# Layer 0's modulation rows: all 32 gate quarters on VectorE, in attention's z tiles and heads c

## The chip, the cores and the metric

The kernel runs on one core of one Trainium2 chip. The metric is the device time of one execution in microseconds (us). The kernel before was timed three times: 3288.5, 3288.59 and 3289.92 us, median 3288.59 us.

## The reference

Two blocks follow each other on x, 256 tokens of width D = 2048. The first mixes three gated branches and ends with a feed-forward network (FFN) of width 5504. The second has two layers of attention over 256 latent and 256 context tokens, with three kinds of heads (a, b, c). The part that the change touches is the adaptive modulation:

```python
sc, scc = jax.nn.silu(c), jax.nn.silu(c_ctx)
for l in range(2):
    shift, scale, gate = jnp.split(sc @ w_ada[l] + b_ada[l], 3, axis=-1)
    shift_c, scale_c, gate_c = jnp.split(scc @ w_ada[l] + b_ada[l], 3, axis=-1)
    h = rms(x, norm_w[l]) * (1.0 + scale[:, None]) + shift[:, None]
    hc = rms(xc, norm_w[l]) * (1.0 + scale_c) + shift_c
    ...   # q, k, v and z from h and hc, three attentions
    x = x + gate[:, None] * merge_out(o_a, o_b, o_c, z, w_out[l])
    if l == 0:
        xc = xc + gate_c * merge_out(oa_c, ob_c, oc_c, z_c, w_out[l])
```

So each layer needs two vectors (for c and for c_ctx) times a matrix of 2048 x 6144. Shift and scale of layer 0 are needed before its projections, its gate only in the output projection out0.

## The kernel before, in words

**The weight stream.** All weights lie in DRAM in the order of use, cut into quarters of 128 partitions x 1024 floats (512 KB). SyncE loads quarter n into slot n % 8 of the ring `raw` once TensorE has counted quarter n - 8 as used (`weights_used`). A matmul quarter is split into two fp32r parts before use: ScalarE copies the high part to `whi` (line 844, ring of 4), VectorE subtracts it and writes the low part `wlo` back into the slot (line 1309). Both run 3 quarters ahead (`AHEAD`). TensorE then makes three matmuls per 128 x 128 chunk (lines 2116, 2117 and 2120 in `tile`; in the wide form lines 2143 and 2144).

**The phases** are listed in `PHASES`, each with its number of quarters and of output tiles. Around the change they are: the FFN's rest group, five FFN groups (g = 0 to 4), and for layer 0 z0, a0, za0, b0, zb0, c0, kvb0, qb0 and out0. An FFN group has 16 up tiles of two quarters and 16 down tiles of one. In group 0 GpSimd also prepares the normalised input of the later groups (lines 2747 to 2754), between the up tiles.

**Modulation on TensorE.** Output columns are taken in blocks of 512, 12 blocks per layer; a block is 8 quarters. These quarters are not split: `mod_quarters` takes them straight from `raw`, two after each tile that has some, with silu(c) in 32-column groups as the stationary operand (line 2172). `weave` and the lists `MOD_FEW` (group 0: 16 quarters, blocks 0 and 1) and `MOD_FFN` (groups 1 to 4: 32 quarters each, four blocks) say after which tile they stand. When a block is complete, VectorE copies its rows (line 1724), TensorE transposes them (`mod_fold`, line 2181), and VectorE adds them up and adds the bias (lines 1733 and 1737).

**Modulation on VectorE.** Blocks 10 and 11, the last half of layer 0's gate, are made in phase c0 (heads c): their 16 quarters hold rows instead, that is 128 outputs on the partitions and half of the 2048 inputs along the row. `gate0_products` (line 1810) multiplies such a quarter with silu(c) and with silu(c_ctx), each spread over all partitions in `crow0`, and sums along the row (`tensor_tensor_reduce`, line 1821): two products per quarter, the product itself thrown into PSUM banks 6 and 7. `crow0` holds one half of the inputs; GpSimd loads the first half at the start of layer 0 (line 2785), and the second once 8 quarters are done (its wait on `gate0_mods`). TensorE waits for the products before a tile's last matmul (`rows_made` in `tile`), as only then it counts the slot as used. Layer 1's gate is made in the same way in out0, with the product thrown into SBUF (line 2070).

**za0 and zb0.** These phases make z tiles (6 and 8 of them, 512 wide), and the attention of heads a and b runs between their matmuls. Each z tile has four slots, one after every four chunks. `beside` puts the pairs of heads into slots: 16 pairs in 24 slots, 24 pairs in 32 slots, starting with slot 2. In a pair's slot p, TensorE makes the scores of p (line 2476), the values of p - 2 (line 2502) and the transposes of p - 1 (line 2487). VectorE's order in a slot is in `z_beside`:

```python
if s % 4 == 2 and s > 2: z_done(...)       # line 1953: gate of the z tile before
if p is a pair: maxima(us[p])              # lines 1904 to 1921
lo(pending)                                # line 1309, every other slot
if p >= 2: gated(us[p - 2])                # line 1947
if p is a pair: norms(us[p])               # waits for ScalarE's exp; lines 1932 to 1938
```

ScalarE makes the exponentials (line 1201) after the maxima and copies the transposed probabilities of the pair before (line 1210). Pairs have by turns 512 keys (latent queries) and 256 keys (context queries). With the slots counted from 0, pairs stand in za0 in slots 2, 4, 5, 6, 7, 9, 10, 11, 12, 14, 15, 16, 17, 19, 20 and 21, and in zb0 in 2, 4 to 9, 11 to 16, 18 to 23 and 25 to 29. Pairs of even number are those with 512 keys.

Of the kernel before, what the change touches and what calls it, by code (L numbers as in the profile page):

```python
# [79 lines left out]
MOD_FEW = [0, 2, 0, 0, 2, 0, 0, 2, 0, 0, 2, 0, 0, 2, 0, 0] + [0] * LATE + [2, 0, 0, 2, 0, 0, 2] + [0] * 6  # L80
MOD_GROUPS = [MOD_FEW if g == 0 else MOD_FFN for g in range(FF_GROUPS)]
# [3 lines left out]
def weave(quarters, mods, before=0, lags=(0, 1, 2)):  # L85
# [21 lines left out]
    assert a % 8 == 0  # L107
# [13 lines left out]
MOD_C = [1, 1, 2, 1, 2, 1, 2, 1, 2, 1, 2]  # L121
C_WEAVE = weave([2] * 11, MOD_C)
C_CHUNKS = sum(MOD_C) // 2
# [6 lines left out]
C_BLOCK = 3 * D // 512 - sum(MOD_C) // 8  # L130
BLOCKS = [*range(C_BLOCK), *range(3 * D // 512, 5 * D // 512)]
assert 8 * len(BLOCKS) == sum(map(sum, MOD_GROUPS)) and sum(MOD_OUT) == 2 * KD and not Z_BEFORE

# [41 lines left out]
def _converted():  # L175
# [3 lines left out]
    for name, nq, _ in PHASES:  # L179
# [3 lines left out]
        elif name in ("z0", "z1"):  # L183
            l = int(name[1])
            own = {pos for e in Z_WEAVE[l] for pos, _ in e["pre"] + e["mods"]}
        elif name in ("c0", "out0"):
            own = {pos for e in (C_WEAVE if name == "c0" else OUT_WEAVE) for pos, _ in e["mods"]}
# [66 lines left out]
def build(nc, stream, xT, ctxT, params, consts, natten, out):  # L254
# [24 lines left out]
    region("gate_mod", 3 * KD * 4)  # L279
# [51 lines left out]
    gate0_half = sb("gate0_half", [2, C_CHUNKS], F32, "gate_mod", 2 * KD * 4)  # L331
# [33 lines left out]
    with ExitStack() as ctx:  # L365
# [225 lines left out]
        def projections(name, l):  # L591
# [700 lines left out]
        def _(vec):  # L1292
# [517 lines left out]
            def gate0_products(e):  # L1810

                for pos, a in e["mods"]:
                    s, (half_, t) = Q0["c0"] + pos, divmod(a, C_CHUNKS)
                    j = 4 * C_BLOCK + t
                    vec.wait_ge(crow0_in, 16 * (half_ + 1))
                    vec.wait_ge(raw_in[s % SLOTS], 16 * (s // SLOTS + 1))
                    for c in range(2):
# [3 lines left out]
                        last = vec.tensor_tensor_reduce(psum[:, 6:8, :].rearrange("p b c -> p (b c)"), raw[:, s % SLOTS, :],  # L1821
# [9 lines left out]
            def projected(name, l):  # L1831
                tiles_, items = projections(name, l)
                for u, (s, nq) in enumerate(t[0:2] for t in tiles_):
                    if name == "a" and l and Z_PAIRS + u <= KD // 2:
                        pair(JOBS_OF["hc1"][0], Z_PAIRS + u)
                    if name == "c" and l == 0 and u < len(C_WEAVE):
                        gate0_products(C_WEAVE[u])

# [118 lines left out]
            def z_beside(kind, l, carry):  # L1957
# [5 lines left out]
                for s in range(4 * n):  # L1963
# [135 lines left out]
        def _(pe):  # L2099
# [4 lines left out]
            def tile(s, d, ts, td, cat, c0, loff, width, nq=2, nch=8, k0=0, ready=None, beside_=None, rows=(), rows_made=None):  # L2104
# [4 lines left out]
                for q in range(nq):  # L2109
# [3 lines left out]
                    for k in range(nch):  # L2113
# [4 lines left out]
                        if rows and q == nq - 1 and k == nch - 1:  # L2118
                            pe.wait_ge(rows_made, rows[-1][1] + 1)
# [279 lines left out]
            def projected(name, l):  # L2399
                tiles_, items = projections(name, l)  # L2400
                first = T0[f"{name}{l}"]
                for u, (s, nq, nch, cat, k0, w) in enumerate(t[0:6] for t in tiles_):
# [9 lines left out]
                    if name == "c" and u == 23:  # L2412
                        cat_ready(JOBS_OF[f"cq{l}"][0])
                    rows = C_WEAVE[u]["mods"] if name == "c" and l == 0 and u < len(C_WEAVE) else ()
                    tile(SQ.index(s), 0, first + u, 0, cat, 0, 2 * S, w, nq=nq, nch=nch, k0=k0, ready=ready,
                         rows=rows, rows_made=gate0_mods)
# [96 lines left out]
            def z_beside(kind, l, carry):  # L2513
# [145 lines left out]
        def _(pool):  # L2659
# [133 lines left out]
            for l in range(LAYERS):  # L2793
# [12 lines left out]
                if l == 0:  # L2806
                    pool.wait_ge(gate0_mods, C_CHUNKS)
# [28 lines left out]
def _stream(w):  # L2836
# [16 lines left out]
    rows = w["w_ada_2"][:, :, 2 * D:].reshape(LAYERS, KD, P, KD, P).transpose(0, 3, 4, 2, 1).reshape(LAYERS, KD, P, 2, QW)  # L2853
# [145 lines left out]
```

## Time and profile before

| what | value |
|---|---|
| median of the runs | 3288.59 us |
| the profiled execution, its time | 3289.74 us |
| its span in the profile | 3287.6 us |
| mean granted TensorE clock | 0.999 of full speed |
| ScalarE, GpSimd busy | 1431.3 us, 614.2 us |
| DMA | 557.67 MB, 170 GB/s mean |
| phases (us from the start of the span) | FFN group 0: 869 to 1006; za0: 1798 to 1897; zb0: 2021 to 2162; c0: 2162 to 2285 |

A row of a timeline has the start, the length, the engine, the line, the operation with output and inputs, a count where several are merged, and in brackets the idle time of the engine before it with what ended it. A row of windows has the stretch, its length, then the busy us (with the number of instructions) of TensorE's matmuls, TensorE's weight loads, VectorE, ScalarE and GpSimd, and last TensorE's granted clock (1.00 is 2.4 GHz, 0.50 is 1.2 GHz), the busy share of DMA and its GB/s. PE is TensorE, DVE VectorE, ACT ScalarE and POOL GpSimd. Matmuls are pipelined, so a matmul's length is longer than the distance to the next.

### The profile page before, as it was taken

Reading aid. Unit: us, or ns where it says so; the run is one execution under the profiler, and the core shown is the slowest. Engines: PE = TensorE matmul, PEld = TensorE weight load, DVE = VectorE, ACT = ScalarE, POOL = GpSimd, SP = SyncE. Lnnn points to the kernel's source line nnn. Section 1 sums busy time; section 2 is a strip of 40 time slices with the busy share of each in tenths; the row PEclk is TensorE's granted clock in tenths of the full one; section 3 lists DMA queues with packets and bytes.
Section 4 is the critical chain, followed back from the end, with each engine's and each line's share of the span. In section 5 each row is a group of like instructions: output and inputs, shape, how many; then the busy total and the mean of one; then the engine's idle time right before and its main releaser. Section 6 shows DMA issues by size and latency. Waiting matters only on the chain.

```text
span 3287.6 us, 56246 instructions
## 1 busy us (share of the span) xinstructions
PE 3251.8 (99%) x20418; PEld 2783.6 (85%) x20418; DVE 2240.7 (68%) x3318; ACT 1431.3 (44%) x2193; POOL 614.2 (19%) x550
## 2 busy tenths in 40 slices
PE   8999999999999999999999999999999999999999
PEld 8999999998987777788888787777868888888978
DVE  7887877567877677677765566567657666774665
ACT  5444445444443343444543433532352363543353
POOL 4999930111440000000300000000001100000000
PEclk9999999999999999999999999999999999999999
DMA  6555555565567777777732222134326533322235
GB/s 219 185 180 183 185 184 185 186 212 182 203 232 253 282 265 279 255 273 263 273 108 101 72 88 78 58 109 148 108 80 214 204 132 111 137 90 96 94 107 171
DMA packets 159583, 557.67 MB, mean 170 GB/s; under 512 B 17520, under 2 KB 23808, under 8 KB 159232
## 3 DMA queue, kind: packets, MB, share of 16 engines
q1 hardware_dynamic: 154144, 534.67, 47.1%
q0 software_dynamic: 5216, 19.94, 1.8%
q8 instruction: 151, 2.47, 0.3%
q14 instruction: 72, 0.59, 0.1%
HBM read 548.23 MB, written 6.31 MB: 169 GB/s over the span
## 4 chain that ended last, share of the span: by engine, by line
PE 94%; DVE 3%; ACT 1%; issue 1%; DVEq 1%; ACTq 0%; DMA 0%; POOL 0%; SPq 0%
PE psum L2116 18%; PE psum L2120 18%; PE psum L2117 18%; PE psum L2143 15%; PE psum L2144 7%; PE psum L2327 4%; PE psum L2476 2%; PE psum L2502 2%; PE psum L2172 2%; PE psum L2487 2%; PE psum L2328 2%; DVE wlo L1309 1%; PE psum L2247 1%; PE psum L2433 1%; DVE rst L1340 0%
## 5 line engine op out<-in xcount | busy, mean ns | idle before, releaser
L844 ACT ACTIVATE whi<-raw 128x1024 fp32r<-128x1024 f32 (+3 forms) x844 | 864.8, 1030 | 1033.7 <-PE psum L2120 571.8
L1309 DVE TENSOR_TENSOR wlo<-raw,whi 128x1024 fp32r<-128x1024 f32 (+3 forms) x844 | 1035.5, 1233 | 398.6 <-ACT whi L844 370.5
L2116 PE MATMUL psum<-hcat,whi 128*128 128x256 f32 (+1 forms) x3436 | 1126.7, 328 | 7.1 <-DVE wlo L1309 6.4
L2120 PE MATMUL psum<-hcat,wlo 128*128 128x256 f32 (+1 forms) x3436 | 1110.6, 323 | 0.0
L2117 PE MATMUL psum<-hcat,whi 128*128 128x256 f32 (+1 forms) x3436 | 1110.4, 323 | 0.0
L2143 PE MATMUL psum<-hcat,whi 128*128 128x512 f32 x2048 | 727.1, 399 | 0.1
L2116 PEld LDWEIGHTS psum<-hcat,whi 128*128 128x128 f32 x3436 | 654.4, 190 | 75.7 <-issue 19.0
L2120 PEld LDWEIGHTS psum<-hcat,wlo 128*128 128x128 f32 x3436 | 654.3, 190 | 51.5
L2117 PEld LDWEIGHTS psum<-hcat,whi 128*128 128x128 f32 x3436 | 654.8, 191 | 49.2 <-issue 0.7
L2144 PE MATMUL psum<-hcat,wlo 128*128 128x256 f32 x2048 | 573.5, 280 | 0.0
L2143 PEld LDWEIGHTS psum<-hcat,whi 128*128 128x128 f32 x2048 | 384.5, 188 | 114.6 <-issue 25.6
L2144 PEld LDWEIGHTS psum<-hcat,wlo 128*128 128x128 f32 x2048 | 386.6, 189 | 0.1
L2675 POOL TENSOR_SCALAR tap<-glu,par 128x255 f32<-128x255 f32 (+9 forms) x150 | 203.6, 1357 | 0.3 <-issue 0.3
L2327 PE MATMUL psum<-thirdcat,whi 128*128 128x512 f32 x512 | 182.4, 400 | 0.0
L2662 POOL TENSOR_TENSOR thirdcat<-tmp,thirdcat 128x256 fp32r<-128x256 f32 x43 | 51.3, 1193 | 634.0 <-ACT thirdcat L898 634.0
L2677 POOL TENSOR_TENSOR conv<-conv,tap 128x255 f32<-128x255 f32 (+9 forms) x150 | 149.3, 995 | 22.1 <-issue 0.3
L2328 PE MATMUL psum<-thirdcat,wlo 128*128 128x256 f32 x512 | 142.8, 279 | 0.0
L2327 PEld LDWEIGHTS psum<-thirdcat,whi 128*128 128x128 f32 x512 | 96.1, 188 | 39.6 <-issue 12.6
L2714 POOL TENSOR_TENSOR racc<-racc,rsq 128x256 f32<-128x256 f32 (+1 forms) x64 | 82.8, 1294 | 236.0 <-ACT rsq L910 209.7
L1340 DVE RECIPROCAL rst<-rst 128x512 f32<-128x512 f32 (+1 forms) x39 | 106.8, 2738 | 27.4 <-ACT rst L873 27.4
L1855 DVE COPY qkv<-psum 128x512 f32<-128x512 f32 (+1 forms) x78 | 49.5, 635 | 111.3 <-PE psum L2120 111.2
L1913 DVE TENSOR_REDUCE stat<-psum 128x2 f32<-128x1024 f32 x78 | 81.6, 1046 | 34.2 <-PE psum L2476 30.2
(297 smaller groups left out, 3568.2 us busy)
## 6 DMA issues: line engine op xcount, KB each, us to landing
raw<-in_stream SPq DMA_DIRECT2D x978, 512.0 KB, 4.3
raw<-in_stream SPq DMA_DIRECT2D x18, 384.0 KB, 3.0
raw<-in_stream SPq DMA_DIRECT2D x24, 256.0 KB, 2.6
resid_dram<-X POOLq DMA_DIRECT2D x2, 2048.0 KB, 9.1
bias<-in_natten POOLq DMA_DIRECT2D x16, 256.0 KB, 3.0
X<-resid_dram POOLq DMA_DIRECT2D x4, 1024.0 KB, 6.1
raw<-in_stream SPq DMA_DIRECT2D x16, 192.0 KB, 2.4
crow<-c_dram POOLq DMA_DIRECT2D x3, 1024.0 KB, 7.3
```

Source lines behind the costliest of these rows:

```text
L844: act.activation(whi[:, c % HI_SLOTS, 0:n], raw[:, slot, 0:n], ACT.Copy).then_inc(hi_ready, 1)
L1309: vec.tensor_tensor(wlo[:, slot, 0:n], raw[:, slot, 0:n], whi[:, c % HI_SLOTS, 0:n].bitcast(F32), ALU.subtract).then_inc(lo_ready, 1)
L1340: vec.reciprocal(r, r)
L2116: pe.matmul(dst, h, cat[:, kk, c0:c0 + width], start=(q == 0 and k == 0), stop=False)
L2117: pe.matmul(dst, h, cat[:, kk, c0 + loff:c0 + loff + width], start=False, stop=False)
L2120: last = pe.matmul(dst, l_, cat[:, kk, c0:c0 + width], start=False, stop=(q == nq - 1 and k == nch - 1))
L2143: pe.matmul(psum[:, bank, :].rearrange("p (l c) -> p l c", l=2), h, both, start=first, stop=False)
L2144: return pe.matmul(psum[:, bank, 0:S], l_, both[:, 0, :], start=False, stop=last)
L2327: pe.matmul(psum[:, bank, :], h, thirdcat[:, kk, :], start=first, stop=False)
L2328: return pe.matmul(psum[:, bank, 0:S], l_, thirdcat[:, kk, 0:S], start=False, stop=last)
L2675: pool.tensor_scalar(tap[:, t % 2, 0:S - t], pick(glu, c, 0, S - t), wt, None, ALU.mult)
L2677: pool.tensor_tensor(pick(conv, c, t, S), pick(conv, c, t, S), tap[:, t % 2, 0:S - t], ALU.add)
```

## The change

The whole gate of layer 0 (blocks 8 to 11, 32 row quarters) is now made by `gate0_products`: 8 quarters in za0, 8 in zb0, and 16 in c0 as before. The first 16 use the first half of the inputs, the 16 of c0 the second. FFN group 0 has no modulation quarters; blocks 0 to 3 are in group 1, 4 to 7 in group 2, 12 to 19 in groups 3 and 4 as before. The number of quarters in the stream stays the same.

In `z_beside` a tile's first row quarter is taken in slot 4t + 1 and its second, where there is one, in slot 4t + 2, after `gated` and before `norms`. The product is thrown into the last two chunks of X in SBUF, which the z tiles fill last. GpSimd waits for 16 quarters instead of 8 before it loads the second half. `ctx_extra` has one more fence (a drain of VectorE) before `gains(0)`.

```diff
-MOD_FEW = [0, 2, 0, 0, 2, 0, 0, 2, 0, 0, 2, 0, 0, 2, 0, 0] + [0] * LATE + [2, 0, 0, 2, 0, 0, 2] + [0] * 6
-MOD_GROUPS = [MOD_FEW if g == 0 else MOD_FFN for g in range(FF_GROUPS)]
+MOD_GROUPS = [[0] * len(MOD_FFN) if g == 0 else MOD_FFN for g in range(FF_GROUPS)]
...
-MOD_C = [1, 1, 2, 1, 2, 1, 2, 1, 2, 1, 2]
-C_WEAVE = weave([2] * 11, MOD_C)
-C_CHUNKS = sum(MOD_C) // 2
+ROW_MODS = dict(za0=[1, 1, 2, 1, 2, 1], zb0=[1] * 8, c0=[1, 1, 2, 1, 2, 1, 2, 1, 2, 1, 2])
+ROW_WEAVE = {name: weave([2] * len(m), m) for name, m in ROW_MODS.items()}
...
+ROW_BLOCKS = [*range(2 * D // 512, 3 * D // 512)] + [5 * D // 512 - 2, 5 * D // 512 - 1]
+ROW_BLOCKS = ROW_BLOCKS[4 - min(ROW_CHUNKS // 4, 4):ROW_CHUNKS // 4 if ROW_CHUNKS > 16 else 4]
+ROW_OF = [4 * b + i for b in ROW_BLOCKS for i in range(4)]
+BLOCKS = [b for b in _blocks if b not in ROW_BLOCKS]
...
             def ctx_extra(t):
                 m = t - 2 * FF_GROUP
                 if t == 0:
+                    fence()
                     gains(0)
...
-            def gate0_products(e):
-
-                for pos, a in e["mods"]:
-                    s, (half_, t) = Q0["c0"] + pos, divmod(a, C_CHUNKS)
-                    j = 4 * C_BLOCK + t
+            def gate0_products(name, e, out, some=slice(None)):
+
+                for pos, a in e["mods"][some]:
+                    s, (half_, t) = Q0[name] + pos, divmod(ROWS0[name] + a, ROW_CHUNKS)
+                    j = ROW_OF[t]
                     vec.wait_ge(crow0_in, 16 * (half_ + 1))
                     vec.wait_ge(raw_in[s % SLOTS], 16 * (s // SLOTS + 1))
                     for c in range(2):
                         start = gate0_half[:, c, t:t + 1] if half_ else pv("b_ada", j)
                         total = ada_t[:, c, j:j + 1] if half_ else gate0_half[:, c, t:t + 1]
                         fence()
-                        last = vec.tensor_tensor_reduce(psum[:, 6:8, :].rearrange("p b c -> p (b c)"), raw[:, s % SLOTS, :],
+                        last = vec.tensor_tensor_reduce(out.rearrange("p b c -> p (b c)"), raw[:, s % SLOTS, :],
                                                         crow0[:, c, :], 1.0, start, ALU.mult, ALU.add, total)
                     last.then_inc(gate0_mods, 1)
...
                     if p is not None and p >= 2:
                         gated(us[p - 2])
+                    if name in ROW_WEAVE and s % 4 in (1, 2):
+                        gate0_products(name, ROW_WEAVE[name][s // 4], X[:, KD - 2:KD, :], slice(s % 4 - 1, s % 4))
                     if p is not None and p < len(us):
                         norms(us[p])
...
+                    rows = ROW_WEAVE[name][t]["mods"] if name in ROW_WEAVE else ()
                     tile(C0[name] + 2 * t, 0, T0[name] + t, 0, hcat, 0, 2 * S, chunks_w(l),
-                         beside_=lambda h: slot(4 * t + h))
+                         beside_=lambda h: slot(4 * t + h), rows=rows, rows_made=gate0_mods, made=ROWS0.get(name, 0))
...
-                    pool.wait_ge(gate0_mods, C_CHUNKS)
+                    pool.wait_ge(gate0_mods, ROW_CHUNKS)
                     crow0_load(1)
```

## Rows read from the trace of the kernel before

**Rows 1.** Busy time of each engine over the whole span, from the page.

```profile
PE 3251.8 (99%) x20418; PEld 2783.6 (85%) x20418; DVE 2240.7 (68%) x3318; ACT 1431.3 (44%) x2193; POOL 614.2 (19%) x550
```

**Rows 2.** Windows: FFN's first group, za0, zb0 (busy us by engine, clock, DMA).

```profile
869.00:1006.00 137.00, 137.00 (x1010) 123.10 (x1010) 110.66 (x163) 57.12 (x76) 54.55 (x52) 1.00 0.69 233
1798.00:1897.00 99.00, 99.00 (x610) 72.29 (x609) 56.17 (x119) 45.96 (x98) 3.23 (x6) 1.00 0.23 75
2021.00:2162.00 141.00, 141.00 (x883) 102.32 (x882) 83.35 (x201) 74.98 (x192) 0.00 (x0) 1.00 0.17 57
```

**Rows 3.** Timeline of TensorE, first group: a pair of modulation quarters between two tiles.

```profile
906.58 0.28 PE L2120 MATMUL psum<-hcat,wlo 128*128 128x256 f32 x1
906.79 1.06 PE L2172 MATMUL psum<-raw,cs 128*32 128x512 f32 x8
...
908.01 0.28 PE L2117 MATMUL psum<-hcat,whi 128*128 128x256 f32 x1
```

**Rows 4.** Timeline of TensorE, first group: a fold between two tiles.

```profile
950.44 0.28 PE L2120 MATMUL psum<-hcat,wlo 128*128 128x256 f32 x1
950.56 0.60 PE L2181 MATMUL psum<-con,arow 128*128 128x128 f32 x4
...
951.11 0.28 PE L2117 MATMUL psum<-hcat,whi 128*128 128x256 f32 x1
```

**Rows 5.** VectorE: line 2070's products (min/median/max ns), and two quarters' products in heads c.

```profile
L2070 DVE CUSTOM_DVE_ANT_0 row_product<-raw,crow,par x16: 1284/1285/2086, 2459.5 to 2595.5; 128x1024 f32<-128x1024 f32 x16
...
2209.43 1.29 DVE L1821 CUSTOM_DVE_ANT_0 psum<-raw,crow,par 128x1024 f32<-128x1024 f32 x1
...
2212.38 1.29 DVE L1821 CUSTOM_DVE_ANT_0 psum<-raw,crow,par 128x1024 f32<-128x1024 f32 x1
```

**Rows 6.** Timeline of VectorE in za0, slots 5, 9 and 10.

```profile
1817.50 0.17 DVE L1934 RECIPROCAL stat<-stat 128x2 f32<-128x2 f32 x1 [1.32 <-ACT probs L1201]
1817.75 0.88 DVE L1938 TENSOR_SCALAR probs<-probs,stat 128x512 f32<-128x512 f32 x2
...
1834.06 0.16 DVE L1934 RECIPROCAL stat<-stat 128x2 f32<-128x2 f32 x1
...
1834.82 0.68 DVE L1953 SCALAR_TENSOR_TENSOR X<-tmp,psum 128x512 f32<-128x512 f32 x1
1837.31 0.70 DVE L1904 SCALAR_TENSOR_TENSOR psum<-bias,psum 128x512 f32<-128x512 f32 x1 [1.80 <-PE psum L2476]
...
1841.41 0.17 DVE L1934 RECIPROCAL stat<-stat 128x2 f32<-128x2 f32 x1 [0.19 <-ACT probs L1201]
1841.66 0.88 DVE L1938 TENSOR_SCALAR probs<-probs,stat 128x512 f32<-128x512 f32 x2
```

**Rows 7.** Timeline of VectorE in zb0, slots 5 and 26.

```profile
2040.54 0.16 DVE L1932 TENSOR_TENSOR stat<-stat 128x2 f32<-128x2 f32 x1 [1.36 <-ACT probs L1201]
...
2041.01 0.88 DVE L1938 TENSOR_SCALAR probs<-probs,stat 128x512 f32<-128x512 f32 x2
...
2138.62 0.43 DVE L1911 TENSOR_TENSOR psum<-psum,con 128x256 f32<-128x256 f32 x1 [1.35 <-PE psum L2476]
```

**Rows 8.** Timeline of TensorE: the transposes that read the probabilities of those pairs.

```profile
1819.21 1.09 PE L2487 MATMUL psum<-con,probs 128*128 128x128 f32 x8
...
1842.77 1.09 PE L2487 MATMUL psum<-con,probs 128*128 128x128 f32 x8
...
2042.15 1.09 PE L2487 MATMUL psum<-con,probs 128*128 128x128 f32 x8
```

**Rows 9.** Timeline of TensorE in z1: its longest wait.

```profile
2648.14 0.58 PE L2116 MATMUL psum<-hcat,whi 128*128 128x256 f32 x1 [3.26 <-DVE wlo L1309]
```

**Rows 10.** Windows right behind that wait; columns as in rows 2.

```profile
2648.00:2654.00 6.00, 5.86 (x28) 5.86 (x29) 5.21 (x7) 3.88 (x8) 0.00 (x0) 0.52 0.03 8
2654.00:2660.00 6.00, 6.00 (x52) 6.00 (x51) 3.69 (x5) 5.62 (x10) 0.00 (x0) 1.00 0.52 175
```

**Rows 11.** Line 2785, loads of crow0: issue to landing.

```profile
DMA to landing us min/median/max: 7.3/9.5/11.6
```

More of the change, by code:

```diff
@@ L120 @@
 Z_PAIRS = 4
-MOD_C = [1, 1, 2, 1, 2, 1, 2, 1, 2, 1, 2]
-C_WEAVE = weave([2] * 11, MOD_C)
-C_CHUNKS = sum(MOD_C) // 2
+ROW_MODS = dict(za0=[1, 1, 2, 1, 2, 1], zb0=[1] * 8, c0=[1, 1, 2, 1, 2, 1, 2, 1, 2, 1, 2])
+ROW_WEAVE = {name: weave([2] * len(m), m) for name, m in ROW_MODS.items()}
+ROWS0, _n = {}, 0
+for _name, _m in ROW_MODS.items():
+    ROWS0[_name] = _n
+    _n += sum(_m)
+ROW_CHUNKS = _n // 2
 MOD_OUT = [0] + [2, 2, 3, 2, 2, 3, 2, 2, 3, 2, 2, 3, 2, 2] + [0]
@@ L185, in _converted @@
             own = {pos for e in Z_WEAVE[l] for pos, _ in e["pre"] + e["mods"]}
-        elif name in ("c0", "out0"):
-            own = {pos for e in (C_WEAVE if name == "c0" else OUT_WEAVE) for pos, _ in e["mods"]}
+        elif name in ROW_WEAVE or name == "out0":
+            own = {pos for e in ROW_WEAVE.get(name, OUT_WEAVE) for pos, _ in e["mods"]}
         of += [Q0[name] + k for k in range(nq) if k not in own]
@@ L1835, in projected @@
                         pair(JOBS_OF["hc1"][0], Z_PAIRS + u)
[L1836 to L1837 removed]
+                    if name == "c" and l == 0 and u < len(ROW_WEAVE["c0"]):
+                        gate0_products("c0", ROW_WEAVE["c0"][u], psum[:, 6:8, :])
                     if u < len(tiles_) - 1 or name != "c":
@@ L2102, in weight, with tile @@
                 return whi[:, c % HI_SLOTS, col:col + n], wlo[:, SQ[c] % SLOTS, col:col + n]
-            def tile(s, d, ts, td, cat, c0, loff, width, nq=2, nch=8, k0=0, ready=None, beside_=None, rows=(), rows_made=None):
+            def tile(s, d, ts, td, cat, c0, loff, width, nq=2, nch=8, k0=0, ready=None, beside_=None, rows=(), rows_made=None, made=0):
                 pe.wait_ge(psum_free, FREE[ts] + td)
@@ L2118, in tile @@
                         if rows and q == nq - 1 and k == nch - 1:
-                            pe.wait_ge(rows_made, rows[-1][1] + 1)
+                            pe.wait_ge(rows_made, made + rows[-1][1] + 1)
                         last = pe.matmul(dst, l_, cat[:, kk, c0:c0 + width], start=False,
@@ L2413, in projected @@
                         cat_ready(JOBS_OF[f"cq{l}"][0])
-                    rows = C_WEAVE[u]["mods"] if name == "c" and l == 0 and u < len(C_WEAVE) else ()
+                    rows = ROW_WEAVE["c0"][u]["mods"] if name == "c" and l == 0 and u < len(ROW_WEAVE["c0"]) else ()
                     tile(SQ.index(s), 0, first + u, 0, cat, 0, 2 * S, w, nq=nq, nch=nch, k0=k0, ready=ready,
-                         rows=rows, rows_made=gate0_mods)
+                         rows=rows, rows_made=gate0_mods, made=ROWS0["c0"])
                 return items[len(tiles_):]
@@ L2862, in put_woven, with put_rows @@
                 put(mods[a_])
+    def put_rows(name, tiles_):
+        if name in ROW_WEAVE:
+            put_woven(ROW_WEAVE[name], tiles_, rows_c[ROWS0[name]:])
+        else:
+            put(tiles_)
     for g in range(-1, FF_GROUPS):
```

33 lines of the change are left out of this document (16 added, 17 removed).

## The prediction

> **What bounds the kernel now.** I read the page first: TensorE is busy for 99% of the span and VectorE for 68% [rows 1], so only what TensorE does or waits for can count. The windows come next, since an average hides stages. In the three stretches that the change touches, TensorE is busy all the time at a granted clock of 1.00, while VectorE works 110.66 of 137 us in the FFN's first group, 56.17 of 99 in za0 and 83.35 of 141 in zb0 [rows 2]. The timelines then show what the spare time of VectorE is made of: in the attention stages it is a relay. TensorE writes scores, VectorE takes maxima, ScalarE exponentials, VectorE normalises (lines 1934 to 1938), and TensorE transposes the result one slot later. VectorE's idle time stands in front of its own parts of the relay [rows 6, 7], and what matters is how long before the transposes [rows 8] it is done.
>
> **What TensorE loses as work.** Blocks 10 and 11 of the modulation leave the first group for line 1821 (its two blocks fall away, as the others shift through the groups). That is 16 quarters, sent in 8 pairs. Around a pair, the third matmul starts 1.43 us after the last of the tile before; at the 0.12 us pitch seen between neighbours [rows 4] it would be 0.24, so a pair costs 1.19 [rows 3], and 8 cost 9.5. A fold costs 0.67 - 0.24 = 0.43 [rows 4], two cost 0.9. **Gain: 10.4 us**, all on the path, as TensorE never idles there.
>
> **What could give some of it back in the first group.** VectorE keeps 110.66 us there less four small mod operations per block (nothing taken for them), in 137 - 10.4 = 126.6 us: 87% instead of 81%. It stays below full, and low halves are made three quarters ahead, which covers single late ones. GpSimd's 54.55 us [rows 2] is squeezed as well, and is far from full. I take 0.3. Below, nothing; above, 3.3, the longest wait of TensorE for a low half that the trace has [rows 9]. DMA demand in the group only falls.
>
> **What VectorE gains as work.** Sixteen more quarters (two products each), 8 in za0 and 8 in zb0. The count in heads c is unchanged. Two products with their fences take 2212.38 - 2209.43 = 2.95 us there, with the result thrown into PSUM; where it goes to SBUF, as now everywhere in attention, one product is 1.285 us [rows 5], so two are at least 2.57. I take 2.95, as it includes fences and accumulator reads. Sum: 47.2 us of work, 23.6 per stage, into 42.8 and 57.7 us of idle. It would fit by sum, so placement decides: each quarter's products stand in slots 4t+1 (and 4t+2 for a tile's second), after the gating and right in front of the normalising of that slot's pair. I walk through the slots.
>
> za0 (24 slots; products in 1, 5, 9, 10, 13, 17, 18, 21):
> - Slot 1 precedes the first pair; slot 13 holds no pair; in slots 17 and 18 the slot without a pair behind takes them up; in 9 and 21 the pair has 256 keys and was ready early. No cost by themselves.
> - Slot 5: VectorE idled 1.32 us before the normalising, so this ends 2.95 - 1.32 = 1.63 later; it ended at 1817.75 + 0.88 = 1818.63 [rows 6] and was wanted at 1819.21 [rows 8]. Slack 0.58, **wait 1.05**.
> - Slots 9 and 10, back to back: in 9 there was no idle, so everything moves by 2.95. The z gating that follows starts at 1837.77 and takes 0.68 and a fence (0.81), so the next maxima start at 1838.58 instead of 1837.31: 1.27 late. Then slot 10's products: 1.27 + 2.95 - 0.19 of idle = 4.03 late, with 1842.77 - 1842.54 = 0.23 of slack [rows 6, 8]. **Wait 3.8**, the largest single one.
>
> zb0 (32 slots; products in 1, 5, 9, 13, 17, 21, 25, 29):
> - Slots 5 and 21: 2.95 - 1.36 = 1.59 late, slack 2042.15 - 2041.89 = 0.26 [rows 7, 8]: **1.33 each**.
> - Slot 25 delays slot 26's maxima, before which VectorE idled 1.35: 1.6 late, slack again 0.26: **1.34**.
> - Slot 13 leaves some 0.2 for slot 14 in the same manner; 1, 9, 17 and 29 nothing (first, or followed by a slot without a pair, or a pair of 256 keys).
>
> Together 4.85 + 4.2 = **9.1 us of new waits** of TensorE. With 2.57 per quarter the same walk gives 6.3.
>
> **Other edits.** In both stages the rows are woven into the weight ring: three quarters per z tile (about 17 us) instead of two, 8 slots, and DMA at 0.23 and 0.17 of its capacity [rows 2]. SyncE's queue issues as many loads as before, 16 of them later, so I cost it at nothing; were this cover gone, ScalarE's copies would start late, at a load's length per tile. TensorE waits for the products before a tile's last matmul, half a tile after they are made: nothing. GpSimd's second load of crow0 now waits for zb0's last product (slot 29) and lands 7.3 us later, at most 11.6 [rows 11]. Two slots of 141/32 = 4.4 us follow slot 29, so it lands before heads c begins or at most some 3 us into it, and TensorE asks for the first products only at the end of a tile that takes longer: nothing. Behind that wait on GpSimd stands the crow load, wanted much later. One fence before gains(0): nothing.
>
> **Sum.** -10.4 + 0.3 + 9.1 = -1.0 us. The profiled execution took 3289.74 us and would take 3288.7; the median of the runs, 3288.59, lies 1.15 lower, and I predict against it: **3287.6 us**. The bounds: 6.3 of waits and no loss in the first group give 3284.5; 3.3 lost there gives 3290.6.
>
> **Rivals.**
> - *The wait of 3.8 us lowers the clock.* After TensorE's longest wait, 3.26 us [rows 9], the granted clock in the next 6 us is 0.52, its lower level of 1.2 GHz for most of it, and 28 matmuls start where 52 do in the 6 us behind [rows 10]. That is 6 - 28 x 6/52 = 2.8 us lost. Slot 10 may do the same: 3287.6 + 2.8 = 3290.4. Against it: the wait is only worked out, and smaller if products are cheaper. The Trainium skill, "TensorE: Matmul & The Clock Gate", section "What's actually happening", says the same in general: the low clock is the default, recent activity releases it. The trace agrees at 0.52. By that rule the time would be this rival's.
> - *VectorE's idle covers the products (faster).* If the relay bends (the 42.8 and 57.7 us are enough by sum) only slot 10 costs something, 2 us: 3288.6 - 10.4 + 2 = 3280. Against it: slacks of 0.23 to 0.58 us.
> - *The lateness is handed on (slower).* Late maxima make ScalarE's exponentials late, these the next scores, so that lateness is not worked off before the next product. Then nine products (slots 5, 9, 10, 21 and 5, 13, 21, 25, 29) cost their whole 2.95: 26.6 of waits, 3288.6 - 10.4 + 26.6 = 3304.8. It ends slower from 17 us of waits on, that is once six products cost in full. Against it: a z tile has 7.1 us of VectorE idle on average, more than one product pair.
> - *The work leaves the first group without its time.* VectorE turns out to set the pace there, and half of the 10.4 stays: 3292.8.
>
> **How the numbers follow.** Forecast 0.42, lower clock 0.27, covered 0.14, handed on 0.12, first group keeps its time 0.05. The first two and the last stay within 0.2% (6.6 us, about what a measurement of this kernel can tell from no change): same 0.74, faster 0.14, slower 0.12. The likeliest case's own range is 3284.5 to 3290.6. The range is stretched towards the covered case below and, past the lower clock with the upper bounds (3293.4), partly towards the handed-on one: 3281 to 3297.
>
> **What would show it.** In the first group no line 2172 or 2181, and some 127 us where there were 137. In za0 and zb0, line 1821 sixteen times two, near 1.29 us each, and waits of TensorE for line 1938 or 1201, one of them near 3.8 us in za0's slot 10, and the granted clock right behind it. za0 longer by about 5 us and zb0 by about 4, heads c unchanged. I am wrong if these stages grow by under 4 or over 17 us together, or if the first group shrinks by under 8.

## The result, and the profile after

The changed kernel takes 3293.85 us (median of 20 runs), the kernel before 3288.56 us (20 runs beside it): a ratio of 1.0015 with a 95% interval of 1.0009 to 1.0021. That is 5.3 us slower. It is inside the 0.2% that the prediction takes for no change and inside its range of 3281 to 3297, but clear of noise and on the other side of the forecast of 1.0 us faster. The profiled execution took 3294.27 us, its span is 3292.4 us, and its mean granted clock is 0.997 (0.999 before). The medians here and below are of fast runs, without two slow ones of e_defer, of 7858.9 and 11268.82 us.

Busy time over the span, from the page of the changed kernel:

```profile
PE 3246.4 (99%) x20346; PEld 2785.5 (85%) x20346; DVE 2277.1 (69%) x3372; ACT 1431.3 (43%) x2193; POOL 615.6 (19%) x550
```

TensorE is busy for 5.4 us less than in [rows 1], about half of the work that left it, and VectorE for 36.4 more. The three stretches of [rows 2], each with the start it has here and the length that was forecast, in windows of the changed kernel (columns as there):

```profile
869.00:996.00 127.00, 127.00 (x942) 121.16 (x941) 108.29 (x152) 57.10 (x77) 54.70 (x52) 1.00 0.54 184
1790.00:1894.00 104.00, 96.22 (x557) 69.10 (x555) 67.45 (x136) 42.70 (x91) 3.23 (x6) 0.95 0.29 102
2018.00:2163.00 145.00, 142.23 (x875) 103.16 (x874) 101.53 (x228) 72.80 (x186) 0.00 (x0) 1.00 0.24 82
```

The first group is what was forecast: TensorE full, VectorE 85% busy (87% was forecast). In zb0 TensorE idles for 2.8 us. The surprise is za0: it idles for 7.8 us there, and the clock is 0.95. TensorE's waits in the changed kernel, longest sums first:

```profile
PE psum L2279 <- DVE wlo L1320: 10.0, 1, 10.0
PE psum L2134 <- DVE gate_half L1833: 7.0, 2, 3.7
PE psum L2130 <- DVE wlo L1320: 6.4, 4, 3.3
PE psum L2501 <- DVE probs L1950: 5.5, 8, 1.1
PE psum L2490 <- ACT probs L1212: 2.6, 3, 1.0
```

The first and third are as old as the kernel. The second is new, and it is the wait that the prediction costed at nothing: line 2134 is a tile's matmul on the low half (2120 before), line 1833 the row product. Its two places, in the timeline of TensorE:

```profile
1834.23 0.39 PE L2131 MATMUL psum<-hcat,whi 128*128 128x512 f32 x1
1838.32 0.77 PE L2134 MATMUL psum<-hcat,wlo 128*128 128x512 f32 x1 [3.70 <-DVE gate_half L1833]
...
1877.34 0.39 PE L2131 MATMUL psum<-hcat,whi 128*128 128x512 f32 x1
1880.98 0.47 PE L2134 MATMUL psum<-hcat,wlo 128*128 128x512 f32 x1 [3.25 <-DVE gate_half L1833]
```

And what VectorE did meanwhile, in its timeline:

```profile
1832.54 1.23 DVE L1925 TENSOR_REDUCE stat<-psum 128x2 f32<-128x1024 f32 x1
...
1835.47 1.28 DVE L1833 CUSTOM_DVE_ANT_0 X<-raw,crow,par 128x1024 f32<-128x1024 f32 x1
1836.68 0.08 DVE L1833 DVE_READ_ACCUMULATOR2_ANT gate_half<- 128x1 f32 x1
1836.88 1.28 DVE L1833 CUSTOM_DVE_ANT_0 X<-raw,crow,par 128x1024 f32<-128x1024 f32 x1
1838.09 0.08 DVE L1833 DVE_READ_ACCUMULATOR2_ANT gate_half<- 128x1 f32 x1
1838.09 0.16 DVE L1946 RECIPROCAL stat<-stat 128x2 f32<-128x2 f32 x1
```

Tile 2 has two row quarters, in slots 9 and 10. TensorE had put out the scores of slot 10 and gone straight on to the tile's last matmuls (the last stands just ahead of slot 11). VectorE finished the maxima of slot 10 at 1834.0, when TensorE was all but there (1834.6), and then made a low half, gated, and had the quarter's products still to do. A quarter's products in slot 4t+2 are made while TensorE is already at the end of the tile. In slot 18 (tile 4) it is the same. Behind both stops the granted clock goes down, in windows of the changed kernel:

```profile
1838.00:1844.00 6.00, 5.68 (x24) 4.12 (x25) 3.07 (x11) 1.79 (x5) 0.00 (x0) 0.52 0.61 225
1844.00:1850.00 6.00, 6.00 (x40) 4.19 (x40) 2.49 (x4) 2.05 (x4) 0.10 (x1) 1.00 0.10 40
1881.00:1887.00 6.00, 6.00 (x30) 4.42 (x31) 2.87 (x7) 2.76 (x7) 0.00 (x0) 0.72 0.66 239
1887.00:1893.00 6.00, 6.00 (x40) 4.20 (x39) 3.56 (x6) 2.34 (x6) 0.00 (x0) 1.00 0.07 26
```

At the full clock 40 matmuls start in 6 us, in the two low windows 24 and 30: 6 - 24 x 6/40 = 2.4 us and 6 - 30 x 6/40 = 1.5 us are lost. That count sets unlike mixes of matmuls side by side. By the granted clock itself it would be 6 x (1 - 0.52) = 2.9 us and 6 x (1 - 0.72) = 1.7 us, the first less some 0.2 for the end of the stop, which lies in its window. So the clock costs 3.9 to 4.4 us in za0, as an estimate. How long the stages take is best read from the first and the last matmul of one kind. The scores of the kernel before (minimum, median and longest in ns, then first and last start), in za0 and in zb0:

```profile
L2476 PE MATMUL psum<-qkv x64: 376/534/693, 1801.4 to 1889.0; 64*128 64x512 f32 x32, 64*128 64x256 f32 x32
...
L2476 PE MATMUL psum<-qkv x96: 376/534/693, 2024.3 to 2153.6; 64*128 64x512 f32 x48, 64*128 64x256 f32 x48
```

The same of the changed kernel:

```profile
L2490 PE MATMUL psum<-qkv x64: 376/589/792, 1793.7 to 1893.7; 64*128 64x512 f32 x32, 64*128 64x256 f32 x32
...
L2490 PE MATMUL psum<-qkv x96: 376/534/693, 2029.0 to 2161.5; 64*128 64x512 f32 x48, 64*128 64x256 f32 x48
```

za0's scores took 87.6 us and take 100.0: **12.4 us longer**, where 4.85 was forecast. zb0's took 129.3 and take 132.5: **3.2 us longer**, where 4.2 was forecast. And za0 starts 7.7 us earlier, not 10.1. The sum of these three terms is +7.9; the spans differ by 4.8, and the last 3.1 come back behind zb0, in stages that the change doesn't touch.

The missing 2.4 us of the FFN have their own story. TensorE waits for GpSimd once just ahead of the FFN, 2.2 us in every kernel here. Windows behind that wait, first of the kernel before:

```profile
843.00:849.00 6.00, 5.96 (x49) 5.96 (x50) 5.11 (x11) 4.70 (x13) 4.29 (x6) 1.00 0.52 172
```

then of the changed kernel:

```profile
843.00:849.00 6.00, 6.00 (x39) 6.00 (x40) 4.95 (x11) 3.94 (x10) 3.94 (x6) 0.72 0.40 135
```

The clock fell in one and not in the other. What the experiments say of that stands below.

### The profile page after: what moved, and what is told of

It is laid out like the page before. It is cut to its first block, busy times and chain, and to the rows that moved or that the text cites. A ratio compares the mean times of both kernels' runs of the same rounds, so it can differ in the third digit from the quotient of the medians.

```text
span 3292.4 us, 56207 instructions
## 1 busy us (share of the span) xinstructions
PE 3246.4 (99%) x20346; PEld 2785.5 (85%) x20346; DVE 2277.1 (69%) x3372; ACT 1431.3 (43%) x2193; POOL 615.6 (19%) x550
## 4 chain that ended last, share of the span: by engine, by line
PE 91%; DVE 5%; ACT 2%; DVEq 1%; issue 1%; ACTq 0%; DMA 0%; POOL 0%; SPq 0%
PE psum L2130 17%; PE psum L2134 17%; PE psum L2131 17%; PE psum L2157 15%; PE psum L2158 7%; PE psum L2341 4%; PE psum L2490 2%; PE psum L2516 2%; PE psum L2186 2%; PE psum L2342 2%; PE psum L2501 2%; DVE wlo L1320 1%; DVE X L1833 1%; PE psum L2261 1%; DVEq L1306 1%
## 5 line engine op out<-in xcount | busy, mean ns | idle before, releaser
L1212 ACT ACTIVATE probs<-psum,stat 128x512 f32<-128x512 f32 (+1 forms) x120 | 72.5, 606 | 78.2 <-DVE stat L1931 78.2
```

## The experiments

**Theory 1** was: the products of a tile's second row quarter make TensorE stop at the tile's last matmul; each stop also lowers the clock; the remaining waits are the ones that the prediction walked through. Its rivals were that the lateness is paid wherever TensorE waits, and that the ring and the queues, not the products, make the time. All kernels start from the changed one. The kernel before was run beside them each time and had medians of 3290.92 us (e_gain, e_short, e_defer, e_both), 3289.55 (e_again, e_one, e_free) and 3289.79 (e_free_own), so the ratios, and not the times, can be set side by side. The table takes its times, read to 0.1 us, from the same rows for each: "FFN" is from the first matmul of the line at which the 2.2 us wait stands (2370, 2356 before; 838.5 in the kernel before, so the wait itself is inside) to the first scores of za0, "group" from that matmul to the first group's last down matmul, za0 and zb0 from first to last scores, and the clock is that of the window 843 to 849.

| kernel | ratio to before (95%) | clock | group | FFN | za0 | zb0 |
|---|---|---|---|---|---|---|
| before | 1 | 1.00 | 166.9 | 962.9 | 87.6 | 129.3 |
| changed | 1.0015 (1.0009 to 1.0021) | 0.72 | 158.3 | 955.4 | 100.0 | 132.5 |
| e_again | 1.0015 (1.0006 to 1.0024) | 0.72 | 158.2 | 955.4 | 100.0 | 132.4 |
| e_gain | 0.9969 (0.9958 to 0.9980) | 0.72 | 158.2 | 954.7 | 87.6 | 129.3 |
| e_short | 0.9972 (0.9961 to 0.9983) | 0.72 | 158.3 | 954.5 | 88.3 | 129.3 |
| e_defer | 0.9997 (0.9988 to 1.0006) | 1.00 | 156.8 | 953.0 | 94.2 | 132.4 |
| e_both | 0.9995 (0.9986 to 1.0004) | 1.00 | 156.8 | 953.6 | 93.8 | 132.4 |
| e_one | 0.9984 (0.9975 to 0.9993) | 0.72 | 158.1 | 954.3 | 89.2 | 132.7 |
| e_free | 0.9968 (0.9956 to 0.9980) | 0.72 | 158.2 | 954.4 | 87.5 | 129.8 |
| e_free_own | 1.0029 (1.0019 to 1.0038) | 0.72 | 158.2 | 954.6 | 99.7 | 136.9 |

**e_gain: the FFN's part alone.**

```diff
-ROW_MODS = dict(za0=[1, 1, 2, 1, 2, 1], zb0=[1] * 8, c0=[1, 1, 2, 1, 2, 1, 2, 1, 2, 1, 2])
+ROW_MODS = dict(za0=[0] * 6, zb0=[0] * 8, c0=[1, 1, 2, 1, 2, 1, 2, 1, 2, 1, 2])
...
-BLOCKS = [b for b in _blocks if b not in ROW_BLOCKS]
+BLOCKS = [b for b in _blocks if b not in range(8, 12)]
...
+            vec.memset(ada_t[:, :, 32:40], 0.0)
```

> The changed kernel without any row product in za0 and zb0: blocks 8 and 9 of the modulation (half of layer 0's gate) are left out and read as zeros, so that the 16 quarters leave the FFN's first group and come back nowhere. Theory 1 (the FFN gives 7.7 us, as the start of za0 moved in the changed kernel's trace; everything over that is lost in za0 and zb0): 3280.9 us, with za0 and zb0 as long as in the kernel before. Theory 2 (the FFN gives the predicted 10.1 to 10.4 us, and some of it is given back only because the new loads wait in SyncE's queue): 3278.3 us. In both the granted clock stays at 1.00 in za0.

Measured: 3280.13 us beside 3290.92 for the kernel before, a ratio of 0.9969, that is 10.2 us less, nearer to theory 2's number (the ratios; by the spans of the two profiled executions it is 8.1). za0 and zb0 are as long as before, with no new wait. The trace shows both theories half right: the first group saves 8.7 us (166.9 to 158.2), and the window behind the 2.2 us wait shows the low clock. In e_defer and e_both, where that window shows 1.00, the group saves 10.1. So the FFN gives 10.1 us, as predicted, and an execution whose clock falls there loses 1.5 of them again. Up to 1.1 more goes between the first group and za0 (FFN less group: 797.1 in the changed kernel, 796.0 before). In the changed kernel most of it stands at three quarters whose first matmul starts late, at 1434.27, 1467.76 and 1473.88, 0.34 to 0.40 us behind its neighbour instead of 0.12; in e_free all three start in step. In e_again and e_both a wait of 0.94 and 0.71 us for GpSimd's queue at 1626 (0.23 elsewhere) is part of it. Why they are late isn't shown.

**e_short: products over 64 of 1024 columns.**

```diff
-                        last = vec.tensor_tensor_reduce(out.rearrange("p b c -> p (b c)"), raw[:, s % SLOTS, :],
-                                                        crow0[:, c, :], 1.0, start, ALU.mult, ALU.add, total)
+                        m_ = QW if name == "c0" else 64
+                        last = vec.tensor_tensor_reduce(out.rearrange("p b c -> p (b c)")[:, 0:m_], raw[:, s % SLOTS, 0:m_],
+                                                        crow0[:, c, 0:m_], 1.0, start, ALU.mult, ALU.add, total)
```

> Every row product in za0 and zb0 stays where it is, with its loads, fences and TensorE's waits for it, but covers 64 of its 1024 columns (the rest of those 16 sums is left out). Theory 1 (the waits are made by VectorE's time in the products): no wait of TensorE over 0.5 us for the products, clock 1.00, some 3282 us, 1 us over the kernel without any products. Rival (the ring and the queues, that is 16 more quarters in these stages, or the semaphore waits themselves, make the time): 3288 us or more, with za0 still at least 6 us longer than before.

Measured: 3281.12 us, ratio 0.9972. One stop for the products is left, 0.5 us, in slot 10, and za0 is 0.7 us longer than before. The 16 extra quarters in the ring, their loads, the fences and the waits cost at most that in za0, and nothing in zb0. The rival falls: it is VectorE's time that costs.

**e_defer: TensorE waits for a tile's products half a tile later.**

```diff
+                        if late_rows and q == 0 and k == nch - 1:
+                            pe.wait_ge(rows_made, made + late_rows[-1][1] + 1)
...
-                            last.then_inc(weights_used, 1 + (len(rows) if q == nq - 1 else 0))
+                            last.then_inc(weights_used, 1 + (len(rows) if q == nq - 1 else 0) + (len(late_rows) if q == 0 else 0))
...
-                    rows = ROW_WEAVE[name][t]["mods"] if name in ROW_WEAVE else ()
+                    rows = ROW_WEAVE[name][t]["mods"] if name in ROW_WEAVE and t == n_ - 1 else ()
+                    late_rows = ROW_WEAVE[name][t - 1]["mods"] if name in ROW_WEAVE and t else ()
```

> TensorE's wait for a tile's row products stands at the end of the next tile's first quarter instead of before the tile's own last matmul; nothing is left out. Theory 1 (the stops of 3.70 and 3.25 us come from that place, and each lowers the clock for some 5 us, which costs 2.4 to 2.8): slot 18's stop and its low clock go, slot 10's becomes a wait of about 3.1 us at the transposes: 3288 us if the clock still falls there, 3285.3 if it doesn't. Rival (the relay is late by the same amount and TensorE meets it wherever it waits): the waits stand at the transposes instead, both of them, and the time stays at 3293 to 3294 us.

The ring slots of the row quarters are given back half a tile later as well. Measured: 3289.62 us, ratio 0.9997, 5.9 us less than the changed kernel (by the ratios). za0 fell from 100.0 to 94.2. The waits of TensorE that are left in za0, in its timeline:

```profile
1811.37 1.09 PE L2503 MATMUL psum<-con,probs 128*128 128x128 f32 x8 [0.82 <-DVE probs L1950]
1834.47 0.70 PE L2492 MATMUL psum<-qkv 64*128 64x256 f32 x4 [0.71 <-ACT probs L1212]
1838.20 1.97 PE L2503 MATMUL psum<-con,probs 128*128 128x128 f32 x8 [2.43 <-DVE probs L1950]
```

Slot 18's stop is gone and nothing stands in its place: it was the wait's position alone. Slot 10's became 0.71 + 2.43 = 3.1 us at scores and transposes, as theory 1 had it, and the clock fell behind it. Windows of e_defer:

```profile
1837.00:1843.00 6.00, 4.80 (x16) 4.13 (x17) 2.80 (x11) 3.48 (x7) 0.00 (x0) 0.50 0.00 0
1843.00:1849.00 6.00, 6.00 (x39) 4.18 (x38) 3.20 (x5) 1.07 (x3) 0.54 (x1) 0.96 0.01 3
```

The rival (same time, other place) falls for slot 18. For slot 10 most of the time is indeed paid in another place, 3.1 of 3.70 us, as theory 1 had it too.

**e_both: both products of a tile in slot 4t+1.**

```diff
-                    if name in ROW_WEAVE and s % 4 in (1, 2):
-                        gate0_products(name, ROW_WEAVE[name][s // 4], X[:, KD - 2:KD, :], slice(s % 4 - 1, s % 4))
+                    if name in ROW_WEAVE and s % 4 == 1:
+                        gate0_products(name, ROW_WEAVE[name][s // 4], X[:, KD - 2:KD, :])
```

> Both row quarters of a two-quarter tile (za0's slots 9 and 17) in slot 4t+1, none in 4t+2; TensorE's wait as in the changed kernel. Theory 1: the products are done before the tile's last matmul, so TensorE doesn't stop there; slot 17 has no pair of its own behind it and costs under 1 us, slot 9 delays its pair by 5.7 us, a wait of 2 to 4.5 us at transposes, with a low clock behind it if it is over 3: 3284 to 3289 us. Rival (lateness is only moved and is paid in full in either place): 3292 to 3296 us.

Measured: 3288.99 us, ratio 0.9995, inside theory 1's range, at its upper end. Two waits take the place of slot 10's stop, in TensorE's timeline:

```profile
1833.16 0.66 PE L2501 MATMUL psum<-con,probs 128*128 128x128 f32 x4 [2.35 <-DVE probs L1950]
...
1837.68 0.70 PE L2490 MATMUL psum<-qkv 64*128 64x256 f32 x4 [1.11 <-ACT probs L1212]
```

and slot 17 still makes TensorE stop at the last matmul, for 1.4 us, where the expectation had no stop and under 1 us. With slot 5's 0.83 that is 5.7 of the 6.2 us that za0 grew by. The clock didn't fall this time, in windows of e_both:

```profile
1832.00:1838.00 6.00, 3.72 (x19) 2.87 (x20) 5.30 (x13) 1.82 (x5) 0.54 (x1) 1.00 0.12 16
1838.00:1844.00 6.00, 6.00 (x40) 3.97 (x38) 2.66 (x9) 3.48 (x8) 0.00 (x0) 1.00 0.72 289
```

So 3.1 us of waits within a few us lowered the clock in e_defer, and 3.5 us of them didn't here. What tells these two apart is left open. The 3 us that the expectation set for a low clock is no mark: the clock fell behind waits of 2.2 and 1.6 us elsewhere (below) and stayed up behind one of 3.25.

**e_again: the changed kernel once more.**

> The changed kernel once more, on the chip of the other experiments. Theory: the low clock right at the FFN's start (one stretch of a granted clock of 0.5, 1.5 us lost) comes and goes between executions, the two low stretches in za0 come every time, as both follow the kernel's own stops: 1.0015 times the kernel before again, +4 to +6 us, za0 longer by 12.4 us and zb0 by 3.2. Rival (za0's low clock was that execution's chance, too): za0 longer by 7 to 8 us only, and the time within 1 us of the kernel before.

Measured: 3294.05 us, ratio 1.0015. za0's stops are 3.71 and 3.25 us with the same two low stretches behind them. The rival falls: they come with the kernel. The low clock ahead of the FFN came again too, so that "comes and goes between executions" isn't shown for this kernel.

**e_one: one row quarter per z tile, 18 in heads c.**

```diff
...
-ROW_MODS = dict(za0=[1, 1, 2, 1, 2, 1], zb0=[1] * 8, c0=[1, 1, 2, 1, 2, 1, 2, 1, 2, 1, 2])
+ROW_MODS = dict(za0=[1] * 6, zb0=[1] * 8, c0=[2, 0, 2, 2, 2, 1, 2, 2, 2, 1, 2])
```

> One row quarter per z tile (6 in za0, 8 in zb0) and 18 in heads c, with the second half of crow0 loaded between heads c's first and third tile; nothing is left out. Theory 1 (second products of a tile make the stops): za0 costs 0.8 us (slot 5), zb0 3.2 as before, clock 1.00 in both, no stop of TensorE for the products; with -10.1 in the FFN the kernel before less 6: ratio 0.998. Rival (heads c becomes the place that pays: crow0 lands after VectorE asks for it, or two products a tile are too many): TensorE waits there, 3 us or more, and the ratio is 0.999 or over.

Measured: 3285.48 us, ratio 0.9984, that is 5.3 us less than the kernel before, where 6 were expected. No stop for the products. za0 pays 0.83 in slot 5 and 0.70 behind slot 9 (the second wasn't expected), zb0 its three waits of 0.80, 0.80 and 0.96. Heads c takes 18 quarters without a new wait.

**e_free: products where the relay has nothing to do.** To e_defer's edit comes

```diff
...
+ROW_MODS = dict(za0=[2, 0, 1, 1, 2, 1], zb0=[2, 0, 1, 1, 1, 0, 1, 1], c0=[2, 0, 2, 2, 2, 1, 2, 2, 2, 1, 2])
+ROW_SLOTS = dict(za0=[1, 3, 8, 13, 17, 18, 21], zb0=[1, 3, 9, 13, 17, 24, 29])
...
-                    if name in ROW_WEAVE and s % 4 in (1, 2):
-                        gate0_products(name, ROW_WEAVE[name][s // 4], X[:, KD - 2:KD, :], slice(s % 4 - 1, s % 4))
+                    if name in ROW_WEAVE and s in ROW_SLOTS[name]:
+                        i = ROW_SLOTS[name].index(s)
+                        gate0_products(name, dict(mods=[m for e in ROW_WEAVE[name] for m in e["mods"]]), X[:, KD - 2:KD, :],
+                                       slice(i, i + 1))
```

> The row products stand where VectorE's relay has no pair, or a pair of 256 keys: slots 1, 3, 8, 13, 17, 18, 21 of za0 and 1, 3, 9, 13, 17, 24, 29 of zb0; 18 quarters in heads c; TensorE's wait at the end of the next tile's first quarter. Nothing is left out. Theory 1 (only the place of the products costs, not their 47 us of work): no new wait of TensorE in za0 and zb0, under 0.5 us each, all of the FFN's 10.1 us kept: ratio 0.997. Rival (the idle time of neighbouring slots is needed by the relay itself, so that lateness is handed on): 3 us or more of waits at transposes and scores, ratio 0.998 or over.

Measured: 3279.28 us beside 3289.55 for the kernel before, ratio 0.9968 (0.9956 to 0.9980): **10.3 us faster than before and about 15 faster than the changed kernel**, with nothing left out. Windows of e_free: za0, zb0, and heads c.

```profile
1790.00:1894.00 104.00, 104.00 (x636) 76.06 (x635) 74.25 (x148) 47.45 (x100) 3.23 (x6) 1.00 0.32 106
2010.00:2160.00 150.00, 149.59 (x927) 108.92 (x926) 105.00 (x238) 77.04 (x195) 0.00 (x0) 1.00 0.24 82
2157.00:2262.00 105.00, 105.00 (x460) 85.54 (x457) 76.73 (x99) 27.27 (x32) 0.71 (x1) 1.00 0.51 177
```

In za0 TensorE is busy for 104.00 of 104 us at a clock of 1.00, where the changed kernel shows 96.22 at 0.95. The 28 products of za0 and zb0 cost 0.5 us in all (zb0: 129.3 to 129.8, one wait of 0.31). e_one has the same 14 quarters in za0 and zb0 and the same 18 in heads c, so the places and TensorE's wait alone make these two stages 4.6 us longer there (89.2 + 132.7 beside 87.5 + 129.8).

Not all of the 10.3 us is the change's. By the last scores of zb0 e_free is 6.2 us ahead of the kernel before (2147.4 and 2153.6), although it starts the FFN 1.8 us later and loses 1.5 to the low clock there. The other 4.1 come where no edit reaches: some 2.2 in z1, where the clock stayed at 1.00 behind [rows 9]'s stop (the prediction worked out a loss of 2.8 us from [rows 10]), and 1.6 in the last 90 us. The stages that the edits touch give 8.1: the FFN 8.5 (10.1 less the clock's 1.5), less 0.4 in za0 and zb0.

**e_free_own: the same slots, TensorE's wait back before the tile's own last matmul.**

```diff
-                    rows = ROW_WEAVE[name][t]["mods"] if name in ROW_WEAVE and t == n_ - 1 else ()
-                    late_rows = ROW_WEAVE[name][t - 1]["mods"] if name in ROW_WEAVE and t else ()
+                    rows = ROW_WEAVE[name][t]["mods"] if name in ROW_WEAVE else ()
```

> The slots of e_free, with TensorE's wait for a tile's products put back before that tile's own last matmul (just ahead of slot 4t+3); nothing is left out. Theory 1 (TensorE stops for every product that stands in slot 4t+2 or later of its tile, one slot ahead of VectorE): exactly three stops, for the products in slots 3 and 18 of za0 and slot 3 of zb0, 3 to 3.8 us each, and none for those in 8, 13, 17, 21, 9, 24, 29; with a low clock behind some of them 9 to 17 us more than e_free: 3288 to 3297 us. Rival (with products in VectorE's idle slots the place of TensorE's wait doesn't matter): within 2 us of e_free, ratio 0.997.

Measured: 3299.40 us, ratio 1.0029, 20 us more than e_free. There are exactly the three stops that were named, and no other. The waits of TensorE in e_free_own:

```profile
PE psum L2136 <- DVE gate_half L1833: 13.9, 3, 5.5
```

They are 5.18, 3.25 and 5.50 us: slot 3's (5.18 and 5.50) are longer than the 3 to 3.8 expected, and the 20 us missed the range of 9 to 17. Around the end of each the clock fell, here in windows of e_free_own, in the order za0 slot 3, zb0 slot 3, za0 slot 18:

```profile
1804.00:1810.00 6.00, 6.00 (x24) 4.45 (x25) 0.66 (x1) 1.54 (x2) 0.00 (x0) 0.73 0.62 197
2039.00:2045.00 6.00, 5.83 (x21) 4.28 (x22) 0.31 (x3) 1.54 (x2) 0.00 (x0) 0.69 0.58 198
1882.00:1888.00 6.00, 6.00 (x31) 4.49 (x31) 2.88 (x7) 2.93 (x7) 0.00 (x0) 0.72 0.64 207
```

This is the run that shows the rule by its positions: products in slot 4t+2 or later of their tile stop TensorE, those in 4t or 4t+1 don't (the second quarter that e_both puts into slot 17 being the one between). In all of these tiles another quarter's products stand one or two slots ahead; a tile with products in slot 4t+2 alone wasn't run.

## Why the prediction was wrong

**The FFN's term was right.** 8 pairs at 1.19 and two folds at 0.43, less 0.3, gave 10.1 us; the first group is 10.1 us shorter wherever the clock stays up in front of it (e_defer, e_both). The 1.5 us that the changed kernel loses there, to a clock that falls behind an old wait of 2.2 us, was in no term: the prediction looked for a low clock behind new waits only. The prediction's upper bound for this group, 3.3 us, rests on a misreading: [rows 9] isn't TensorE's longest wait for a low half, which is the one at the start of the span, 9.7 us (10.0 in the changed kernel).

**The step that failed** is "TensorE waits for the products before a tile's last matmul, half a tile after they are made: nothing". It holds for slot 4t+1. The products of a tile's second quarter stand in slot 4t+2, and the last matmul is asked for one slot behind it on TensorE's own count; but VectorE works a slot behind TensorE in this relay, so nothing lies between. So two stops stand there: 3.70 us in slot 10, and 3.25 us in slot 18, which the walk had passed as free because no pair follows it. With the low clock behind them they cost 10.9 to 11.4 us, where the sum had 3.8 for slot 10 and nothing else: enough to turn 1.0 faster into slower. e_defer shows that 3.25 us were position alone, and e_free_own finds the rule again in slot 18 and in two new places, slot 3 of za0 and of zb0. The profile before could have told. VectorE's gating and TensorE's last matmul of the tile, in the timelines of VectorE and TensorE of the kernel before, first slot 10, then slot 18 (there the gate of the z tile stands last):

```profile
1840.94 0.28 DVE L1947 TENSOR_TENSOR X<-psum,X 128x128 f32<-128x128 f32 x1
1841.23 0.39 PE L2120 MATMUL psum<-hcat,wlo 128*128 128x512 f32 x1
...
1876.09 0.68 DVE L1953 SCALAR_TENSOR_TENSOR X<-tmp,psum 128x512 f32<-128x512 f32 x1
1877.93 0.39 PE L2120 MATMUL psum<-hcat,wlo 128*128 128x512 f32 x1
```

In slot 10 the products could start at 1841.22 at the earliest, where TensorE wants them done at 1841.23. In slot 18 there are 1877.93 - 1876.77 = 1.2 us for 2.7 us of work, even if slot 17's products delayed nothing.

**The lower clock, a rival with 0.27, happened**, twice instead of once, at 2.4 and 1.5 us by the count of matmuls where 2.8 had been worked out from [rows 10]. The Trainium skill, "TensorE: Matmul & The Clock Gate", section "What's actually happening", has the low clock as the default that recent activity lifts. The trace agrees after stops of 3.25 to 5.5 us in za0 and zb0, each followed by a window at 0.52 to 0.73. It doesn't behind the stop of 3.25 us in e_free's z1, followed by one at 1.00. By itself this rival's 3290.4 would have been too fast: it had the clock and not the second stop.

**The relay's waits were right in place and a little large.** Slot 5: 1.05 forecast, 0.83 measured. zb0: slots 5, 21 and 26 at 1.33, 1.33 and 1.34, measured 0.79, 0.80 and 0.97; slot 14 at 0.2, measured 0. One term was a little too large: from one quarter's first product to the next quarter's it is 2.95 us in [rows 5], and 1872.83 - 1869.99 = 2.84 in e_both's slot 17, as the accumulator read behind a product takes 0.08 us where its result is thrown into SBUF and 0.14 where it is thrown into PSUM. (From the first product to the end of the last read it is 1838.17 - 1835.47 = 2.70.) That explains 0.1 us of each wait and not the rest. The slot 10 wait of 3.8 is 0.71 + 2.43 = 3.1 in e_defer, and in the changed kernel the stop at the last matmul took its place; that this one has nearly the size forecast for the other is luck. The lower bound has a slip: with 2.57 per quarter the same walk gives 0.67 + 3.04 in za0 and 0.95 + 0.95 + 0.96 in zb0, 6.6 us and not 6.3.

**The other edits** cost next to nothing, as forecast: e_short bounds ring, loads, fences and semaphores in za0 and zb0 at 0.7 us, and heads c keeps TensorE full even with two quarters more.

**The rivals on VectorE.** "Covered" gave 3280 for the case that the idle time is enough. It wasn't true of the changed kernel. In e_free, with two of the 16 quarters moved to heads c and the others in other slots, the stages do cover the products; that its 3279.3 us meets the rival's number is in part luck, as 4.1 us of it come from stages that no edit reaches. "Handed on" fell: TensorE's new waits stand within a slot or two of products, and none elsewhere.

**The sum, corrected**: -10.1 for the FFN, +1.5 and up to 1.1 given back on the way to za0 (-7.5 in the table), +7.8 of waits and 3.9 to 4.4 of clock in za0 (12.4 in all, so 0.2 to 0.7 has no place), +3.2 in zb0: +8.1. Behind zb0 3.1 us come back, 1.0 of it in z1, behind [rows 9]'s stop (from there to the next long wait 129.6 us before, 128.7 now), 1.6 in the last 90 us, and the rest ahead of z1's stop. The 1.6 aren't the change's doing: from TensorE's last long wait (1.17 us at line 2516, 2502 before) to the end it is 91.6 us in the kernel before and also in e_short, e_defer, e_both and e_one, which have the change's schedule of the FFN, and 90.0 in the changed kernel and the other four. The prediction's own signs of being wrong didn't show, as za0 and zb0 grew by 15.6 us together (17 was its mark) and the first group shrank by 8.6 (8).

## What to carry to other kernels

When work is added to an engine that is a link of a relay, its total idle time says little: go through the schedule's slots, put the work in those where the relay is empty, and cost it at nothing only there. For each semaphore wait that the added work brings, compare when the waiting engine gets there with when the working engine can be done, in time and not in slot numbers, since the two engines stand at different slots at the same moment. And a stop of TensorE costs what the clock loses behind it as well, where it falls: in the changed kernel stops of 3.25 and 3.70 us cost 4.8 and 6.1, by the count of matmuls.

## What was not expected of the hardware

- **The clock falls behind short waits, but not each time.** Behind the 2.2 us wait ahead of the FFN it fell in 7 of 10 traces (the changed kernel and its repetition among them; not in the one of the kernel before, e_defer and e_both). Behind a wait of 1.6 us some 28 us ahead of z1's stop (line 2206 of the changed kernel) it fell in four: the changed kernel (0.72 from 2628 to 2634), e_again, e_defer and e_one. Behind the stop of 3.3 us in z1 it stayed up only in e_free. The two windows of e_free around that stop:

```profile
2637.00:2643.00 6.00, 2.75 (x23) 2.55 (x22) 5.06 (x7) 5.87 (x11) 0.00 (x0) 1.00 0.48 163
2643.00:2649.00 6.00, 6.00 (x52) 6.00 (x51) 5.43 (x9) 5.71 (x10) 0.00 (x0) 1.00 0.28 98
```

  In [rows 10] the window right behind it shows 0.52 and 28 matmuls. So two kernels can differ by 1.5 us ahead of the FFN and by 2.2 in z1 (from the stop to the next long wait 129.6 us in the kernel before, 127.5 in e_free), places that neither touches, and a difference of that size needs the windows behind every stop compared before it is put down to an edit.

- **Stretches that no kernel changes run 2% slower in some of them.** From 760 to 800 us, at a clock of 1.00 and without a wait, the kernel before starts 233 matmuls and the changed one and its repetition 232. The kernel before:

```profile
760.00:800.00 40.00, 40.00 (x233) 35.28 (x232) 29.82 (x37) 20.20 (x31) 5.86 (x8) 1.00 0.58 193
```

  e_free:

```profile
760.00:800.00 40.00, 40.00 (x228) 34.67 (x227) 29.08 (x36) 19.02 (x28) 5.47 (x7) 1.00 0.55 184
```

  228 or 229 stand there in all of e_gain, e_short, e_defer, e_both, e_one, e_free and e_free_own. It isn't the chip, since e_again ran on the same one as e_one and e_free. It costs (233 - 228) x 40/233 = 0.9 us in these 40, and some 1.7 us in all, as 494 matmuls start from 718 to 803 in the kernel before and 484 in e_free. The last 90 us have the same, in other kernels: from 3215 to 3255 us 228 or 229 matmuls start in the kernel before, e_short, e_defer, e_both and e_one, and 232 or 233 in the other five. No run shows a cause.
